# Moving the buffers that TensorE reads by 32 to 224 bytes, each by its own amount

## The reference

```
proj = rms_norm(x, norm_in_g) @ w_in                 # 1024 x 6144
q, k, v, g_ret, x_lru, g_lru = split(proj)
y_ret = group_norm(chunkwise_retention(rot(q), rot(k), v)) * silu(g_ret)
y_lru = rg_lru(conv(x_lru), gates) * silu(g_lru)
x = rms_norm(x + concat(y_ret, y_lru) @ w_out, norm_out_g)

for l in range(2):                                   # on 256 tokens and 256 context tokens
    h = modulate(rms_norm(x), sh1, sc1)
    z = h @ w_in_2[l]                                # mLSTM, grouped and windowed attention, gates
    o = merge(mlstm(z), grouped_attention(z), window_attention(z)) @ w_out_2[l]
    x = x + ga1 * rms_norm(o)
    f = conv_ffn(modulate(rms_norm(x), sh2, sc2), w_up[l], w_down[l])
    x = x + ga2 * rms_norm(f)
```

## Time and profile before

| | |
|---|---|
| median of 3 timed runs | 1667.76 us (1667.32 to 1667.93) |
| span of the profiled execution | 1666.5 us, 1.3 us under that median |
| PE busy | 1654.8 us, 9,772 matmuls, clock 1.00 throughout |
| VectorE, ScalarE busy | 1234.7 and 856.6 us |
| matmuls of 512 columns in float32r, full array | 4,584 |
| of 256 columns in float32r, full array | 2,976 |

### The profile page before, as it was taken

One profiled execution on the slowest core, in us unless ns is written; L12 is line 12 of the kernel. 1 busy time (PEld: TensorE's weight loads), 2 busy tenths in 40 slices (PEclk: granted clock), 3 DMA queues, 4 the chain that ended last, 5 costly groups with the idle time before them and its releaser, 6 DMA issues.

```text
span 1666.5 us, 25155 instructions
## 1 busy us (share of the span) xinstructions
PE 1654.8 (99%) x9772; PEld 1421.7 (85%) x9772; DVE 1234.7 (74%) x2143; ACT 856.6 (51%) x1403; POOL 0.2 (0%) x4
## 2 busy tenths in 40 slices
PE   9999999999999999999999999999999999999998
PEld 9898888778887778889888888888778999989997
DVE  7999967966777897857887775347756776677874
ACT  7776655554334443356444442347553455576653
POOL 0000000000000000000000000000000000000000
PEclk9999999999999999999999999999999999999999
DMA  8668743232235345523545556324422344555563
GB/s 332 236 204 276 247 142 106 66 125 77 66 107 187 110 151 203 195 95 128 136 178 182 187 183 221 99 76 142 112 76 76 124 160 148 190 164 175 180 205 124
DMA packets 80230, 258.02 MB, mean 155 GB/s; under 512 B 14448, under 2 KB 18800, under 8 KB 79472
## 3 DMA queue, kind: packets, MB, share of 16 engines
q1 hardware_dynamic: 74352, 248.02, 44.9%
q10 hardware_dynamic: 5760, 8.39, 1.5%
HBM read 255.31 MB, written 1.07 MB: 154 GB/s over the span
## 4 chain that ended last, share of the span: by engine, by line
PE 86%; DVE 7%; ACT 3%; issue 2%; DMA 1%; ACTq 0%; DVEq 0%
PE bank L800 72%; PE bank L994 3%; PE bank L1172 2%; PE bank L1188 2%; DVE w_lo L2056 2%; PE bank L1160 2%; PE bank L1268 2%; DMA w_raw<-in_weights 1%; DVE mod_w L2111 1%; ACT w_hi L1380 1%; PE bank L1254 1%; PE bank L837 0%; DVE junk_gate L2111 0%; DVE ptmp L2454 0%; DVE probT L2111 0%
## 5 line engine op out<-in xcount | busy, mean ns | idle before, releaser
L2056 DVE TENSOR_TENSOR w_lo<-w_raw,w_hi 128x1024 fp32r<-128x1024 f32 (+1 forms) x356 | 427.6, 1209 | 255.6 <-ACT w_hi L1380 254.4
L1380 ACT ACTIVATE w_hi<-w_raw 128x1024 fp32r<-128x1024 f32 (+1 forms) x356 | 370.4, 1049 | 333.7 <-PE bank L800 286.5
L800 PE MATMUL bank<-hT_hi,w_hi 128*128 128x512 f32 (+1 forms) x1280 | 446.6, 349 | 0.0
L800 PE MATMUL bank<-hT_hi,w_lo 128*128 128x512 f32 (+1 forms) x1280 | 437.6, 342 | 0.0
L800 PE MATMUL bank<-hT_lo,w_hi 128*128 128x512 f32 (+1 forms) x1280 | 437.4, 342 | 0.0
L800 PEld LDWEIGHTS bank<-hT_hi,w_lo 128*128 128x128 f32 x1280 | 242.5, 189 | 28.2
L800 PEld LDWEIGHTS bank<-hT_hi,w_hi 128*128 128x128 f32 x1280 | 242.6, 190 | 28.0 <-issue 1.7
L800 PEld LDWEIGHTS bank<-hT_lo,w_hi 128*128 128x128 f32 x1280 | 242.8, 190 | 27.2 <-issue 1.0
L2111 DVE SCALAR_TENSOR_TENSOR mod_w<-mod_w,c_rows 128x1024 f32<-128x1024 f32 x102 | 124.2, 1217 | 7.2 <-DMA mod_w<-in_mod_weights 7.0
L800 PE MATMUL bank<-w_hi,hT_hi 128*128 128x512 f32 x272 | 114.3, 420 | 0.0
L800 PE MATMUL bank<-w_lo,hT_hi 128*128 128x512 f32 x272 | 106.7, 392 | 0.0
(11 more groups left out here) (415 smaller groups left out, 2708.9 us busy)
## 6 DMA issues: line engine op xcount, KB each, us to landing
w_raw<-in_weights SPq DMA_DIRECT2D x356, 512.0 KB, 4.3
mod_w<-in_mod_weights SPq DMA_DIRECT2D x102, 512.0 KB, 3.9
nbias<-in_window_bias ACTq DMA_DIRECT2D x32, 128.0 KB, 3.3
resid_c<-in_ctx ACTq DMA_DIRECT2D x2, 1024.0 KB, 6.0
gain_mix<-gain_rows SPq DMA_DIRECT2D x3, 512.0 KB, 5.4
gain_ffn<-gain_rows SPq DMA_DIRECT2D x3, 512.0 KB, 4.1
c_rows<-in_conditions SPq DMA_DIRECT2D x1, 1024.0 KB, 8.9
gatew<-in_gate_weights SPq DMA_DIRECT2D x1, 1024.0 KB, 11.3
```

Source lines behind the costliest of these rows:

```text
L800: mm = pe.matmul(held[key][:, oc], st, mv_, start=(opens and k == 0 and t == 0 and i == 0), stop=(closes and k == tiles - 1 and t == 2), s ...
L1380: a.activation(w_hi[:, p % RING, :, used], w_raw[:, p % RING, :].rearrange("p (k n) -> p k n", k=KP)[:, :, used], ACT.Copy).then_inc(hi_re ...
L2056: v.tensor_tensor(w_lo[:, p % RING, :, used], w_raw[:, p % RING, :].rearrange("p (k n) -> p k n", k=KP)[:, :, used], w_hi[:, p % RING, :, ...
```

## The change

Four amounts are added to the offsets: 32 bytes for the low half of the rows and what shares its place, and for `w_raw`; 96 for `w_hi`; 160 for `w_lo`; 224 for R and so for everything from R on, C's tables included. `hT_hi`, `xT_hi`, `xT_lo` and the residual rows stay. No instruction is added, removed or moved.

```diff
+LOW_AT, WHOLE_AT, REST_AT, STAGE_AT = 32, 96, 160, 224
...
     hT_hi = sb("hT_hi", [P, 2, KD, T], 16 * KB, F32R)
-    hT_lo = sb("hT_lo", [P, 2, KD, T], 32 * KB, F32R)
-    w_raw = sb("w_raw", [P, RING, KP * COLS], 48 * KB)
-    w_hi = sb("w_hi", [P, RING, KP, COLS], 64 * KB, F32R)
-    w_lo = sb("w_lo", [P, RING, KP, COLS], 80 * KB, F32R)
-    R = 96 * KB
+    hT_lo = sb("hT_lo", [P, 2, KD, T], 32 * KB + LOW_AT, F32R)
+    w_raw = sb("w_raw", [P, RING, KP * COLS], 48 * KB + LOW_AT)
+    w_hi = sb("w_hi", [P, RING, KP, COLS], 64 * KB + WHOLE_AT, F32R)
+    w_lo = sb("w_lo", [P, RING, KP, COLS], 80 * KB + REST_AT, F32R)
+    R = 96 * KB + STAGE_AT
     C = R + 88.0625 * KB
...
-    gatew = sb("gatew", [P, 2, HEADS, P], 32 * KB)
-    xc = sb("xc", [P, HEADS, T], 40 * KB)
+    gatew = sb("gatew", [P, 2, HEADS, P], 32 * KB + LOW_AT)
+    xc = sb("xc", [P, HEADS, T], 40 * KB + LOW_AT)
...
-    o_ffn = [sb("o_ffn_c", [P, NT, D], 24 * KB), sb("o_ffn_x", [P, NT, D], 40 * KB)]
+    o_ffn = [sb("o_ffn_c", [P, NT, D], 24 * KB), sb("o_ffn_x", [P, NT, D], 40 * KB + LOW_AT)]
```

## The result

| | before | after |
|---|---|---|
| median of 4 runs of each | 1667.54 us (1667.10 to 1667.93) | 1680.99 us (1680.63 to 1681.77) |
| ratio of the medians | | 1.008, 95% interval 1.0065 to 1.0094 |
| span of the profiled execution | 1666.5 us | 1678.8 us |

The change costs 13.45 us between the medians and 12.3 us between the profiled spans. The page of the kernel after answers to the earlier trace rows: span, busy time by engine, granted clock, the chain by engine.

The account below looks back on a forecast made before the run. PE bounds the kernel, busy 99% of the span. Terms of +24.4 and -3.6 us gave +20.8 on PE, nine tenths of it +18.7: span 1685.2, median 1686 us; range 1642 to 1702 us, 8 times in 10.

Parts of the forecast that it names:

- the ring: Weight transfers land 4.3 us after issue into a ring of four; a start 32 bytes further moves nothing there.
- mg as the witness: mg, loaded 64 bytes off while w streams in 144 matmuls, steps at 233 ns against 227: unequal remainders are dearer.
- No effect: Rival: mg's dependence is peculiar to it, other remainders keep steps of 227 and 120 ns; 1667 to 1668 us, chance 0.15.
- The term for 512 columns: Full-array float32r matmuls of 512 columns: 5.5 ns more for each of 4,440, +24.4 us.
- The term for 256 columns: 2,976 matmuls of 256 columns: about the same cost or 1.2 ns less each, -3.6 us.
- the 272-column form: Nearest in size to 256 columns, without one settled pattern: 125.4 ns a step, a fixed part of 12.1 against 13.3.
- a sign of being wrong: 256- and 512-column groups becoming shorter than 283 and 389 ns would show equal remainders were the collision.
- nine tenths: Share of PE's +20.8 us taken to reach the span, as 14% of the chain is not PE's: +18.7 us.
- slower: Case that steps lengthen as mg's do: 1686 us, chance 0.47, plus a dearer version at 1714 to 1725 us, 0.05.
- Faster: Rival: equal remainders collide and make part of the 13.3 ns; -22 us, 1645 us, chance 0.33.
- the scores: Attention scores, 64 rows run in pairs: 390 ns at unequal remainders against 393 at equal, so 3 ns cheaper.
- 13.3 isn't a floor: The fixed part of a step, 13.3 ns at 256 and 512 columns, can be lower, as the 272-column form's 12.1 shows.

Follow-up runs that it names:

- weights by 64: Against the kernel before, w_hi and w_lo stand 64 bytes further, R and all behind it 256; 1670.63 us, ratio 1.0022.
- all by 32: Against the kernel before, all buffers stand 32 bytes further, differences within pairs unchanged; 1667.67 us, ratio 1.0.
- weights by 32: Against the kernel before, w_hi and w_lo stand 32 bytes further, R and all behind it 256; 1686.65 us in one run.
- chosen version: Against the kernel before: w_hi, w_lo and R +256, xT +192, mg's .0625 removed, last wide layer's hT rows under second names +192; 1658.70 us, ratio 0.9944.

## Why the prediction was right, and where its numbers were off

**What bounds it.** PE did, and still does: its busy time took all of the change (+13.2 us), and the others' waits for it grew by 8.8 and 10.2 us. That the ring and the engines behind it cover the shifts of w_raw and of their own operands was right: their busy times and the transfers' wait did not move.

**mg as the witness.** This was the step that decided the sign, and it held. The weights by 64 put the 6 ns on the other buffers and took them off mg. "No effect" fell with the first trace. Between all by 32 (227.6 ns) and weights by 32 (233.2 ns) what differs by 256 is where w_hi and w_lo stand to everything else. The Trainium skill (SBUF — State Buffer, "Who interferes with whom") gives PE two independent read ports; taken to mean that the place of one operand cannot cost the other time, these rows do not agree with it. Whether the ports themselves are where the time is lost, no run shows.

**The term for 512 columns** was mis-sized: "I take it for all: 5.5 ns by 4,440". The steps rose by 4.0 ns with rows streamed and by 3.8 with weights streamed, mg's included, which is 3.9 x 4,584 = 17.9 us in place of 24.4. That a price read at a difference of 64 alone came within 2 ns of the mean over the changed kernel's mixture is in part luck: by pair the rise goes from 1.2 to 6.5 ns. The one price hid two things. The pairs of after are not one kind:

```
streamed, loaded next     difference   step of 512 columns
hT_hi, w_hi                    96            232.9
hT_lo, w_lo                   128            228.7
w_hi, fT_hi                   128            228.4
w_hi, fT_lo                   128            231.7
w_lo, fT_hi                    64            233.3
w_hi, hT_hi                   160            235.3
w_hi, hT_lo                   192            231.4
w_lo, hT_hi                    96            231.5
```

And a pair's step depends on the others in its product: 128 costs 1 ns here (hT_lo, w_lo) and 5 in the kernel with weights by 128. The prices "of 0, 64, 96, 128 and 160", which the prediction wanted to read "one by one from the groups", can't be read so. It also said 394 to 397 ns for the groups; they are 390 to 396, and 389 became 393 for fT_hi.

**The term for 256 columns**, -1.2 ns from the 272-column form, came out at -0.9: 119.8 to 118.9 ns, -2.7 us. It lies in xT and yT (117 to 118 ns), whose group did become shorter than 283 ns (280 for xT_hi past w_lo), one half of what the prediction named as a sign of being wrong; hT stayed at 119.3 and 120.4, and the last layer at 119.9. The idea behind it was better than the number: a stream that loses its pattern at 256 columns is cheaper, and with one at 64 bytes much cheaper.

**What the waits absorb.** The two terms as measured are 17.9 - 2.7 = 15.2 us, and the span grew by 12.3: 0.81, where "nine tenths" was taken. The factor came near, its reason did not: PE's waits, where a slower PE should wait less, add up to 5.2 us before and 4.3 after in the view of waits, which is 0.9 of the 2.9 us. The trace says where the rest is. The undisturbed steps gave +16.5 us at 512 columns and -2.8 at 256; the other 320 or so of 512 columns, beside small work or a wait, did not grow, and all steps besides the undisturbed ones, these and the small work's, became 1.3 us shorter together. With the prediction's own factor and these sizes the sum would have been 1666.5 + 0.9 x 15.2 + 1.3 = 1681.5 us.

**The range.** 1642 to 1702 us takes in both signs, and slower had a chance of 0.52 against 0.33 for faster. That the time fell inside says little; what was right is the sign, from mg, and a size of +18.7 us where 12.3 (spans) and 13.5 (medians) were measured.

**"Faster"** was a real mechanism at another place. Its witness, the scores, are two row groups at once and said nothing of the full array at 512 columns, where no shift tried was cheaper than none. It was a weak one even among the scores. A second form of the kernel before whose operands also have the difference 0 takes the 390 ns that were read as the gain of unequal remainders:

```profile
L1160 PE MATMUL bank<-gkT_hi,gqT_lo 64*128 64x512 f32 x32 | 6.4, 390 | 0.0
```

But "13.3 isn't a floor" was true at 256 columns: the chosen version runs at a fixed part of 113.4 - 106.7 = 6.7 ns. The rival priced it at 3 ns for every matmul and both sizes; it is up to 6.7 at one size and nothing at the other. The 2.5 ns that the Trainium skill (TensorE: Matmul & The Clock Gate, "Back-to-back issue gap") gives for isolated matmuls were reached in no stretch of these runs.

## What to carry to other kernels

Where PE bounds and each matmul has its own weight load, read the steps from the timeline by size and pair before touching the layout, and look for a pair that the kernel already runs at another remainder: such an exception is a free experiment. Of the shifts tried here, operands that agree by 256 bytes were best at 512 columns and 64 bytes between weights and rows at 256 columns, and the whole set of a product's operands counts, so shifts must be tried as a set and not added up. At 64 bytes and 256 columns a stream can settle at 113 or at 118 ns in the same kernel: look at every execution's time before taking one trace for the kernel. A shift that makes one stream faster is worth little where the next weights are not there yet.

## What was not expected of the hardware

The settled steps named here are whole multiples of 6.67 ns, 16 cycles of 2.4 GHz, or become so over two or three steps: 120.0 ns is 18 of them, 113.3 is 17, 226.7 is 34; three of 117.8 are 353.3, or 53; mg's pair of 231 and 236 is 466.7, or 70; fT's three in the kernel after are 693.3, or 104, against 680, or 102, before. These multiples are worked out from the starts in the traces. They fit with the fixed part of 13.3 and 6.7 ns being two and one of such slots, but what hands out these slots no run shows. The same remainders and the same buffers gave 117.8 and 113.3 ns at 256 columns within one execution, and what chooses is open. Differences under 32 bytes were not tried.
